# A four-layer decoder step on one core: new order of the first mixer's products, seven cache slots, and another path from router to experts

## The reference

```python
def trunk(x, pos0, mem_k, mem_v, ssm, ssm_conv, ret, pool, conv, p):
    for l in range(DEPTH):                       # DEPTH = 2
        h = rmsnorm(x, p['norm_mix'][l])
        m = even_mixer(h, ...) if l % 2 == 0 else odd_mixer(h, ...)
        x = x + m
        x = x + cross_attn(rmsnorm(x, p['norm_cross'][l]), mem_k[l], mem_v[l], ...)
        h = rmsnorm(x, p['norm_ffn'][l])
        x = x + (swiglu(h, ...) if l % 2 == 0 else moe(h, ...))   # moe: top 2 of 8 experts
    return rmsnorm(x, p['norm_final'])

def even_mixer(...):   # the first mixer
    z, xbc, dt, q, k, v, g = jnp.split(h @ w_in, offs, axis=-1)
    ...                # convolution of xbc; a state space scan gated by z; a retention of q, k, v gated by g

def cross_attn(h, mk, mv, wq, wo):
    q = (h @ wq).reshape(bsz, seq, X_HEADS, X_HEAD_DIM)
    s = jnp.einsum('blhd,bmhd->bhlm', q, mk) * (X_HEAD_DIM ** -0.5)
    p = jax.nn.softmax(s, axis=-1)
    return jnp.einsum('blhm,bmhd->blhd', p, mv).reshape(...) @ wo
```

## Time and profile before

| | before |
|---|---|
| time, median of 3 runs | 1542.44 us (1539.12 to 1542.48) |
| the profiled execution | 1542.72 us, span 1540.2 us |
| PE busy | 1442.6 us, 94% |
| DVE, ACT, POOL busy | 468.0, 206.2, 125.6 us |
| granted PE clock, mean | 0.954 of 2.4 GHz |
| DMA | 368.26 MB, mean 239 GB/s |

### The profile page before, as it was taken

One profiled execution on the slowest core, in us unless ns is written; L12 is line 12 of the kernel. 1 busy time (PEld: TensorE's weight loads), 2 busy tenths in 40 slices (PEclk: granted clock), 3 DMA queues, 4 the chain that ended last, 5 costly groups with the idle time before them and its releaser, 6 DMA issues.

```text
span 1540.2 us, 22151 instructions
## 1 busy us (share of the span) xinstructions
PE 1442.6 (94%) x9354; PEld 999.2 (65%) x9354; DVE 468.0 (30%) x1300; ACT 206.2 (13%) x430; POOL 125.6 (8%) x156
## 2 busy tenths in 40 slices
PE   7999989999998999999999998949999999999991
PEld 5887667788875888888887866734444444444440
DVE  3345656530361211412299344220000000000003
ACT  2121112201211100000103121130000000000001
POOL 3003413400010200000000001020000000000001
PEclk9998979899998999999999988869999999999996
DMA  9643634655393896444444468537999999999962
GB/s 281 213 154 96 173 96 145 211 183 169 120 354 135 286 400 198 130 142 141 162 144 152 145 229 314 208 133 299 383 398 381 386 403 361 365 405 344 390 239 95
DMA packets 184057, 368.26 MB, mean 239 GB/s; under 512 B 8420, under 2 KB 117244, under 8 KB 183809
## 3 DMA queue, kind: packets, MB, share of 16 engines
q1 hardware_dynamic: 162600, 292.47, 53.2%
q0 software_dynamic: 19264, 71.23, 13.3%
q10 hardware_dynamic: 2096, 3.15, 0.6%
HBM read 339.13 MB, written 28.49 MB: 239 GB/s over the span
## 4 chain that ended last, share of the span: by engine, by line
PE 91%; DVE 3%; DMA 3%; issue 2%; POOL 1%; ACT 1%; SPq 0%; ACTq 0%; POOLq 0%; DVEq 0%
PE psum L887 33%; PE psum L1433 13%; PE psum L1299 10%; PE psum L1196 7%; PE psum L1439 7%; PE psum L1472 6%; PE psum L1478 3%; DMA ring<-in_cache_mem_v_dram 1%; PE psum L1238 1%; PE psum L1263 1%; PE psum L1230 1%; DMA expert_rows<-arena 1%; PE psum L1450 1%; PE psum L996 1%; PE psum L912 0%
## 5 line engine op out<-in xcount | busy, mean ns | idle before, releaser
L887 PE MATMUL psum<-hT,ring 128*128 128x264 f32 x1168 | 276.6, 400 | 1.1 <-ACT hT L1515 1.1
L887 PEld LDWEIGHTS psum<-hT,ring 128*128 128x128 f32 x1168 | 228.5, 197 | 49.4 <-issue 7.1
L887 PE MATMUL psum<-arena,ring 128*128 128x264 f32 x992 | 227.3, 392 | 1.5 <-ACT arena L1673 0.8
L887 PEld LDWEIGHTS psum<-arena,ring 128*128 128x128 f32 x992 | 191.3, 194 | 35.8 <-issue 1.2
L1299 PE MATMUL psum<-hT,ring 128*128 128x264 f32 x704 | 157.1, 386 | 0.0
L1299 PEld LDWEIGHTS psum<-hT,ring 128*128 128x128 f32 x704 | 133.7, 190 | 22.8
L1433 PE MATMUL psum<-ring,arena 128*64 128x384 f32 (+1 forms) x704 | 137.2, 541 | 0.0
L1196 PE MATMUL psum<-ring,arena 128*128 128x256 f32 x512 | 115.3, 386 | 0.0
L1196 PEld LDWEIGHTS psum<-ring,arena 128*128 128x128 f32 x512 | 98.5, 194 | 18.9 <-issue 5.3
L1798 DVE TENSOR_TENSOR arena<-psum,rstd 128x264 f32<-128x264 f32 (+3 forms) x117 | 43.7, 393 | 206.6 <-PE psum L1299 111.0
L1433 PEld LDWEIGHTS psum<-ring,arena 128*64 128x64 f32 x704 | 49.1, 137 | 79.9 <-issue 79.9
(11 more groups left out here) (432 smaller groups left out, 1221.7 us busy)
## 6 DMA issues: line engine op xcount, KB each, us to landing
ring<-in_moe_w_dram SPq DMA_DIRECT2D x72, 1024.0 KB, 16.8
arena<-in_moe_w_dram SPq DMA_DIRECT2D x40, 1024.0 KB, 14.6
ring<-in_moe_w_dram SPq DMA_DIRECT2D x44, 768.0 KB, 15.0
ring<-in_ffn_w_dram SPq DMA_DIRECT2D x30, 1024.0 KB, 5.4
ring<-in_w_in_even_dram SPq DMA_DIRECT2D x22, 1024.0 KB, 5.6
ring<-in_cache_mem_k_dram POOLq DMA_DIRECT2D x16, 1024.0 KB, 8.1
ring<-in_cache_mem_v_dram POOLq DMA_DIRECT2D x16, 1024.0 KB, 6.3
arena<-in_moe_w_dram SPq DMA_DIRECT2D x20, 768.0 KB, 16.2
```

The source lines that it names most:

```text
L887: ins = mm(outs_[m][0:mw, 0:T], wv[:, k, m * mw:(m + 1) * mw], rhs(base + k), start=(base + k == 0), stop=(kc == len(chunks) - 1 and k == ...
```

## The change

Seven edits, in the order of the program:

1. First mixer: four of the eight v tiles are computed later, two behind the sample transposes and two behind the first decay rows (with the input already scaled, so DVE copies them only); the z blocks are computed a tile at a time (`one_tile`), one ahead of and one behind the sample product 2s; the sample product 2s+1 moves ahead of the rotations; the transposes of the samples' v move ahead of those of y.
2. The last g block is split: one tile behind sample 4, one behind sample 5.
3. Five cache slots become seven, in both attentions. The two new ones are the end of the arena, which are the first two slots of the expert weights. In the second layer they are loaded once the second mixer is done there.
4. The transposes of the prompt's attention weights move ahead of samples 6 and 7, and ACT copies them out in place of DVE.
5. Two of the four copies of `sums_out` go to DVE.
6. The router's weights are loaded ahead of the second attention; the final norm's gain keeps its place and gets another semaphore.
7. All of the first ten expert loads are issued at `aos_done`. The first expert's rows are not loaded from DRAM: DVE makes a 0/1 matrix `chosen0` (token by place), and PE multiplies the tokens with it. The six stores stay, for the other experts.

```diff
-KV_SLOTS = RING - TRUNK_RING
+KV_RING = RING - TRUNK_RING
+KV_SLOTS = KV_RING + 2
...
+        kv = [X[:, i * 2 * DM:(i + 1) * 2 * DM].rearrange("p (m d) -> p m d", m=2) for i in range(KV_RING)]
+        kv += [view(arena_n - (2 - i) * 2 * DM, 2, DM) for i in range(2)]
...
-            full(sp, ("wout1", KT - 1))
-            sp.wait_ge(sem("odd_out"), 64)
-            for j in range(2):
-                expert_load(0, j, j)
...
             sp.wait_ge(sem("aos_done"), 2)
-            for j in range(5, 10):
+            for j in range(10):
                 expert_load(0, j, j)
...
             sp.wait_ge(sem("rows_out"), 96)
-            rows_load(0)
...
-            taken(pool, ("v", RH - 1))
+            taken(pool, ("v", 3))
             nc.gpsimd.tensor_tensor(hT[:, :, :], hT[:, :, :], rstd[:].unsqueeze(1).to_broadcast([P, KT, T]), ALU.mult)\
                 .then_inc(sem("h_scaled"), 1)
...
-            linear("v", 4, [8], h_in)
+            linear("v", 2, [8], h_in)
+
+            def one_tile(name, t):
+
+                i = item_at[(name, t // 2, 0)]
+                arrived(i)
+                wv = slot_view(i % TRUNK_RING, 8, 256)
+                o = begin((name, t))
+                for k in range(KT):
+                    ins = mm(o[:, 0:T], wv[:, k, t % 2 * P:(t % 2 + 1) * P], hT[:, k, :], start=(k == 0), stop=(k == KT - 1))
+                end((name, t), ins)
...
+            pe.wait_ge(sem("h_scaled"), 1)
+            linear("v", 1, [8], h_in, first=2)
             pe.wait_ge(sem("ead_ready"), 1)
...
             decay_rows(0)
+            linear("v", 1, [8], h_in, first=3)
...
+                one_tile("z", 2 * s)
                 sample_x(2 * s)
-                if s == 0:
-                    pe.wait_ge(sem("h_scaled"), 1)
-                linear("z", 1, [8], h_in, first=s)
+                one_tile("z", 2 * s + 1)
...
                 sample_v(b)
-                if b == 4:
-                    linear("g", 1, [8], h_in, first=3)
+                if b in (4, 5):
+                    one_tile("g", b + 2)
...
-            pe.wait_ge(sem("rows_in"), 16)
-            turn_rows()
+            pe.wait_ge(sem("picked_ready"), 2)
+            for j in range(2):
+                for t in range(4):
+                    for c in range(3):
+                        n = P if c < 2 else NB
+                        ins = mm(psum[:, (5, 2)[j], t * CAP:(t + 1) * CAP], htok[0:n, c, (4 * j + t) * P:(4 * j + t + 1) * P],
+                                 chosen0[0:n, c, :], start=(c == 0), stop=(c == 2), skip_group_check=True)
+                if j == 0:
+                    ins.then_inc(sem("turned_low"), 1)
+            ins.then_inc(sem("rows_turned"), 1)
...
+                dve.wait_ge(sem("aos_done"), l + 1)
+                for j in range(2, 4):
+                    ins = v.tensor_copy(aor[0:NB, j * 256:(j + 1) * 256], psum[32 * j:32 * j + NB, SUMS, 0:256])
+                ins.then_inc(sem("sums_out"), 1)
...
+            for c in range(3):
+                n = P if c < 2 else NB
+                ins = v.tensor_scalar(chosen0[0:n, c, :], const("iota")[0:n, :], slot[0:n, c, 0:1], picked[0:n, c, 0:1],
+                                      ALU.is_equal, ALU.mult)
+            ins.then_inc(sem("picked_ready"), 1)
```

More of the change, by code:

```diff
@@ L799, in _ @@
             memload()
-            for n in range(KV_SLOTS):
+            for n in range(KV_RING):
                 kvload(1, n)
@@ L821, in _ @@
             memory_k_out(1)
+            taken(pool, ("pw", OT - 1))
+            nc.gpsimd.memset(rwt[:, :, :], 0.0).then_inc(sem("blank_set"), 1)
+            pool.wait_ge(sem("blank_set"), 2)
+            load(rwt[:, :, 0:NE], w["router_w"][0].rearrange("(t p) e -> p t e", p=P), "router_in")
+            load(rbt, w["router_b"].to_broadcast([P, NE]), "router_in")
+            pool.wait_ge(sem("odd_out"), 64)
+            taken(pool, ("pw", OT - 1))
+            taken(pool, ("var",))
+            for n in range(KV_RING, KV_SLOTS):
+                kvload(1, n)
             more_kv(1)
@@ L1061, in _ @@
                     end(("rot", i), mm(o[:, 0:T], const("rot"), qk[:, i, :], start=True, stop=True))
-                sample_x(2 * s + 1)
+            for t in range(RH):
+                taken(pe, ("v", t))
+            for j in range(2):
+                o = begin(("vstok", j))
+                for t in range(4):
+                    ins = tr(o[0:NB, t * P:(t + 1) * P], vT[:, 4 * j + t, NP:T], ident)
+                end(("vstok", j), ins)
             sample_y(NB - 1)
@@ L1571, in _, with sums_out @@
                 gate_out("z", 2 * s)
-            def sums_out(dst, n, width):
-                for j in range(4):
+            def sums_out(dst, n, width, parts=range(4)):
+                for j in parts:
                     ins = af(dst[0:n, j * width:(j + 1) * width], psum[32 * j:32 * j + n, SUMS, 0:width], ACT.Copy)
@@ L1870, in _, with values @@
             v.tensor_copy(acT[0:SH, NP:T], na[:, NP:T]).then_inc(sem("dt_steps"), 1)
-            for t in range(RH):
-                full(dve, ("v", t))
-                free(("v", t), scaled(vT[:, t, :], bank(("v", t))[:, 0:T]))
+            def values(tiles):
+                for t in tiles:
+                    full(dve, ("v", t))
+                    out, now = vT[:, t, :], bank(("v", t))[:, 0:T]
+                    free(("v", t), scaled(out, now) if t < 4 else v.tensor_copy(out, now))
+            values(range(4))
             full(dve, ("dtT",))
@@ L1977, in _ @@
                     dve.wait_ge(sem("rot_done"), i + 1)
-                sample_state(2 * s + 1)
+            for j in range(2):
+                full(dve, ("vstok", j))
+                free(("vstok", j), v.tensor_copy(vstok[0:NB, j * 512:(j + 1) * 512], bank(("vstok", j))[0:NB, :]))
             for t in range(KT):
```

113 lines of the change are left out of this document (51 added, 62 removed).

## The result

The changed kernel takes 1500.9 us, the median of four runs (1492.66 to 1504.02), against 1540.88 us for the kernel before (four runs, 1539.12 to 1542.48): the ratio is 0.9732 with a 95% interval of 0.9689 to 0.9776. The forecast was 1494 with a range of 1480 to 1512. The profiled execution took 1498.76 us around a span of 1497.0, so the spans to compare are 1540.2 and 1497.0, 43.2 us apart; the sum in the prediction was 48.8.

The account below looks back on a forecast made before the run. PE, busy 94% of 1540.2 us, was taken as the bound, losing time where it stands or runs at half clock. Gains 16 + 2.5 + 15.3 + 15 = 48.8 off 1542.7 gave 1494 us, range 1480 to 1512.

Parts of the forecast that it names:

- First mixer, v and z: First mixer, v products to first g product: late v and split z tiles cover waits; gain 16 us, 2.5 deducted for clock.
- Rival A: First mixer gives only 5 us, since the sample chain or the falling clock sets the pace; 1505 us, chance 0.20.
- The last g block: First mixer's end: cut in two, each half covers one state update; gain 2.5 us, ends 0 and 4.
- Both attentions: Both attentions: seven slots bring value rows sooner, copies and sums move; gain 15.3 us together, ends 5 and 19.
- Rival C: Attentions: extra slots fail, row 7 lands as late as before, behind the values' store; 1505 to 1509 us, chance 0.06.
- The router and the join: Projection to experts: early router loads gain 8.3 us, the gather replaces stores and load; 15 us together, ends 9 and 18.
- the weight of three to one for a warm gather: Router: full-clock gather (17.0 us in all) weighed three to one over half clock (9.6), as no wait over 2 us remained.
- the cold case: Router: gather at the half clock takes 11.3 us, experts start at 1035.7; gain 9.6 us in all.
- Two signs of being wrong: Among the signs listed: first-mixer windows of 0.50 between 115 and 205, and gather products over 0.2 us each.
- rival B: Router: the gather costs as much as at the half clock; 1501 us, chance 0.10.
- Expert weights: Ahead of the experts: five of sixteen loads move later, still covered by about 10 us; else 2.7 us per load.
- Rival D: Expert loop becomes bound by its transfers, so slower; gain gone below 352 GB/s, 1554 us at 345; chance 0.02.

Follow-up runs that it names:

- the kernel with fillers: The changed kernel plus three 128x512 products that nothing reads, put in PE's waits ahead of the picked experts and the gather: 1501.92 us.
- wide_gather: The changed kernel with the 0/1 matrix as weights and tokens moving, 12 instructions of 512 columns, ahead of the last residual transposes: 1490.02 us.

## Why the prediction was right, and where it was not

**First mixer, v and z.** Right in cause and size: 16.7 us for 16. PE's longest wait there is 0.74 us, the z tiles run at 1.00, and the fall of the clock that was deducted came behind the loop, at 203. One reading was wrong: not 2 to 4 us but 7.4 us of other products stand between the last z tile of a turn and the first of the next (y, kv, sample product, rotations and decay rows, 143.84 to 151.25), and the clock stayed at 1.00 there. Rival A is out.

**The last g block.** Right in kind, too large by the run that undoes it: 0.9 us for 2.5. Two waits of 1.2 and 0.9 us stay (L1115 in the list of waits). The first stands ahead of the block, for sample 3, where the split changes nothing; the second is for sample 7, behind which no g tile is left. One wait of 1.05 us is gone.

**Both attentions.** Right: 16.9 us for 15.3. The rows were to take 8.5 us and take 7.8 and 8.3, with one wait each (0.5 and 1.1 us). The slots give 11.3 by the run with five (forecast 11.7), copies and sums 4.0 (forecast 3.6); 1.6 us are left that neither run gives back. Missing in the sum were 3.4 us in the stretches behind both attentions (2.2, and 9.5 less the 8.3 of the wait). In this execution the clock stood at 0.50 for less of the projections. Of the ten profiled kernels with these short waits seven took 421.4 us from the first projection to the second attention and three 423.0 to 424.5, where the kernel before took 423.6; so how much of the 3.4 us is the change's and how much the execution's stays open. Rival C is out.

**The router and the join.** The term of the sum that failed: 15 us forecast, 4.6 measured (8.3 of wait, less 2.3 and 1.4), below its own low end of 9. The early loads were right, 8.3, and the run without them lost 7.9. The step that failed is the weight of three to one for a warm gather, "PE now has no wait of over 2 us from projection to experts". The prices were some 10% low: 0.13 us an instruction at the full clock, 12.5 us at mostly half (forecast 0.118, and 11.3 at half). But no long wait does not mean that the clock is kept. It fell in the rank and the residual transposes, which the second profile of the same kernel runs in 5.6 us at 1.00 and the first in 7.8; it fell again in the gather, which began at 1.00 each time; and it made the first expert block 10.0 us. Nor did the cold case count the residual transposes and the longer first block. Two signs of being wrong that the prediction named came: windows of 0.50 ahead of 205 (from 203 on), and gather instructions of over 0.2 us (0.26 on average). So rival B came true in its mechanism. Its 1501 does not follow from the prediction's own cold case, which has 9.6 us in place of 15 and so gives 1499; that the time measured is 1500.9 is in part luck, by offsetting terms: the router is 10.4 us short of its term, the other terms and the start are 4.8 us over. 48.8 - 10.4 + 4.8 = 43.2.

The Trainium skill, "TensorE: Matmul & The Clock Gate", section Terms, names a transpose mode on trn2 that is four times faster for FP32, from which the prediction worked out 12.5 us and the same 1501, an estimate. The gather did take 12.5 us, but for another reason. At 1.00 eight transposes of 96 columns take 0.85 us, 0.11 each, and a gather product of two instructions 0.26, so 2.4 times; the second half of the 12.5 us is the clock.

**Expert weights.** Right: no wait on them is in the list. Rival D is out; the loop moved 391 GB/s in the window that starts 23 us behind the first expert product, 394 in the like window before, and lost only what the first block lost. The Trainium skill, "DMA: Bandwidth & Descriptors", section Bandwidth, names about 358 GB/s for a core when both cores of its HBM domain stream, a condition that the prediction left out. This kernel runs on one core, and its trace shows 391, that of before 394.

## What to carry to other kernels

An exchange of a transfer for PE work must be priced at the clock that PE will have there, and a stretch of small products had no claim to the full one here, even without a wait (0.50 for 10 of the 12.5 us of the gather). When rows were picked by a 0/1 matrix here, the form with few instructions of many moving columns was cheaper, and the clock stayed at or rose to 1.00 in it (12 instructions of 512 columns in 5.9 to 6.6 us, against 48 of 96 in 11.0 to 13.6), though it also stood at another place in PE's order. Judge single edits of a few us by the stretch they touch, when the runs of one kernel lie 11 us apart.

## What was not expected of the hardware

PE at 0.50 with no gap in its work: in the kernel with fillers the clock fell 3.9 us into 48 instructions of 128x96, and in wide_gather it rose from 0.50 to 1.00 within two us of the start of 12 instructions of 128x512. The same instructions with nearly the same waits took 65.8 to 72.0 us in one stretch of the first mixer, by the place where the clock fell. Four runs of the changed kernel lie 11 us apart, four of the kernel before 3.4.
